# Key, value and expert-weight transfers laid out in other runs, and the token sort done through DRAM: one inference step on one core

## The reference

```python
h = modulate(rmsnorm(x, g_attn), shift, scale)
fq, fk, fv, logf, mq, mk, mv = project(h, w_in, b_forget)
o = merge_groups(fox(...), moba(...), g_out_fox, g_out_moba, w_out)   # 8 + 8 heads of 64
x = x + gate * o
h = modulate(rmsnorm(x, g_ffn), shift2, scale2)
# top-1 of 4 groups, then top-2 of the 8 experts in it; expert e on row h:
y_e = (silu(h @ w1[e]) * (h @ w3[e])) @ w2[e]      # w1, w3: 1024x256, w2: 256x1024
x = x + gate2 * (weighted sum of the two y_e);  y = rmsnorm(x, g_final)
```

## Time and profile before

| | us |
|---|---|
| runs | 919.58, 927.25, 929.08 |
| median | 927.25 |
| profiled execution | 922.37 |
| its span | 920.6 |
| PE busy | 675.6 |
| DVE busy | 398.9 |
| granted TensorE clock, mean | 0.832 |

### The profile page before, as it was taken

How to read it: one execution, slowest core, us unless ns; L and a number is a source line. 1 busy time by engine, 2 the same in 40 slices (tenths; PEclk the granted TensorE clock), 3 DMA queues, 4 the chain that set the end, 5 groups by cost and what they waited for, 6 DMA issues and landing times.

```text
span 920.6 us, 13094 instructions
## 1 busy us (share of the span) xinstructions
PE 675.6 (73%) x4650; PEld 376.1 (41%) x4650; DVE 398.9 (43%) x824; ACT 171.3 (19%) x438; POOL 170.0 (18%) x209
## 2 busy tenths in 40 slices
PE   4699999966464666566668978997777777687740
PEld 2356466444232333233335765444343434343410
DVE  1412112155877577576874237123323232323226
ACT  2011002048121111111202123121101111111013
POOL 2201203330044444454420000010000000000010
PEclk9899999977776765776769977999988898988885
DMA  9996779560585966866478080009999999999944
GB/s 324 405 379 185 278 297 365 184 240 1 167 296 208 320 222 203 322 218 211 129 262 275 1 275 0 1 29 369 378 369 378 368 378 368 378 369 378 370 127 131
DMA packets 126700, 233.77 MB, mean 254 GB/s; under 512 B 8626, under 2 KB 74347, under 8 KB 126532
## 3 DMA queue, kind: packets, MB, share of 16 engines
q1 hardware_dynamic: 105330, 176.70, 53.9%
q0 software_dynamic: 13232, 41.27, 13.8%
q10 hardware_dynamic: 8098, 15.28, 4.8%
HBM read 217.96 MB, written 15.25 MB: 253 GB/s over the span
## 4 chain that ended last, share of the span: by engine, by line
PE 32%; SPq 25%; DVE 21%; DMA 6%; issue 6%; another core or an unknown queue 5%; ACT 2%; ACTq 0%; DVEq 0%; POOL 0%; POOLq 0%
SPq L478 13%; SPq L479 11%; PE ps L1588 8%; DVE work L1144 5%; PE ps L1592 5%; PE ps L1885 4%; PE ps L1810 4%; DMA ring<-w_in 3%; SPq L477 2%; DVE p_half L1215 2%; PE ps L1898 2%; PE ps L1483 2%; PE ps L1692 1%; DMA ring<-w 1%
## 5 line engine op out<-in xcount | busy, mean ns | idle before, releaser
L1898 PE MATMUL ps<-ring,work 128*64 128x256 f32 x1024 | 148.6, 455 | 40.7 <-DMA ring<-w 39.5
L1898 PEld LDWEIGHTS ps<-ring,work 128*64 128x64 f32 x1024 | 87.4, 164 | 94.3 <-issue 70.8
L1383 DVE TENSOR_SCALAR work<-work 128x128 f32<-128x128 f32 x32 | 15.7, 490 | 214.4 <-ACT work L837 214.4
L1692 PE MATMUL ps<-work 128*32 128x256 f32 x512 | 55.5, 580 | 52.5 <-DVE work L1144 52.5
L563 POOL DMA_INDIRECT ring<-cache_moba_v,v_row x64 | 60.5, 946 | 140.1 <-PE ps L1737 116.5
L586 POOL COPY work<-work 128x512 f32 x32 | 19.6, 614 | 337.2 <-PE ps L1898 240.8
L1588 PE MATMUL ps<-xh,ring 128*128 128x320 f32 x256 | 73.7, 447 | 6.3 <-DMA ring<-w_in 6.3
L563 POOL DMA_INDIRECT ring<-cache_fox_v,v_row x64 | 60.7, 948 | 90.4 <-PE ps L1483 38.2
L1144 DVE STREAM_TRANSPOSE work<-ring 128x2048 f32<-128x2048 f32 x32 | 71.8, 2285 | 0.0
L1588 PEld LDWEIGHTS ps<-xh,ring 128*128 128x128 f32 x256 | 49.7, 197 | 28.7 <-DMA ring<-w_in 6.6
L1907 PE MATMUL ps<-ring,work 128*64 128x512 f32 x256 | 60.6, 593 | 0.7 <-ACT work L841 0.4
(11 more groups left out here) (318 smaller groups left out, 867.1 us busy)
## 6 DMA issues: line engine op xcount, KB each, us to landing
ring<-w SPq DMA_DIRECT2D x96, 1024.0 KB, 12.7
ring<-w_ada SPq DMA_DIRECT2D x4, 4096.0 KB
ring<-cache_fox_k SPq DMA_DIRECT2D x64, 256.0 KB
ring<-cache_moba_k SPq DMA_DIRECT2D x64, 256.0 KB
ring<-w_ada SPq DMA_DIRECT2D x4, 2048.0 KB, 13.8
ring<-w_in SPq DMA_DIRECT2D x2, 4096.0 KB
scr_y<-work ACTq DMA_DIRECT2D x64, 128.0 KB, 5.6
ring<-w_in SPq DMA_DIRECT2D x2, 2048.0 KB
```

The lines of the kernel that those rows point to most:

```text
L1692: last = mm(o.rearrange("p (q n) -> p q n", q=2), q_cur[:, u.g, 2 * h + e, :], ktv[:, :, 2 * h + e, :], start=(e == 0), stop=(e == 1))
L1898: last = mm(o, h_cur[:, par, c, :], w[:, c, f], start=(c == 0), stop=(c == KC - 1))
```

## The change

1. **Keys.** Token 4l + t of a page now goes to partition 32t + l. The transfer's DRAM side is therefore a pattern of 4 by 32 rows of 512 floats (outer step one row, inner step four rows); the SBUF side stays 128 partitions of 512.
2. **Values.** Partition 32a + l takes tokens 4l to 4l+3 of page a as one run of 8 KB, so that a unit has two indirect transfers in place of eight. The log-forget values, the bias tables and the suffix sums follow the new order of tokens.
3. **Expert weights.** w1 and w3 are loaded with eight neighbouring input rows per partition, one run of 8 KB, and each has a region of its own in the slot.
4. **Sort.** DVE casts the places to integers, POOL scatters the rows of `h_tok` to `scr_h` in DRAM with six indirect transfers, SP reads the sorted rows back in two transfers, and PE turns them with 40 transposes, which ACT and DVE evacuate. The one-hot matrices, their matmuls and POOL's iota go.
5. **Router.** The logits of the two prompt tiles are accumulated chunk by chunk as the activations come, into banks of their own; only the sample tile is left for the end. Some semaphores are merged.

```diff
--- before.py
+++ after.py
@@ -129,6 +129,7 @@
+    scr_h = nc.dram_tensor("scr_h", (ASSIGN, D), F32).ap()
@@ -148,7 +149,9 @@
-        w13_of = [s[:, 0:2 * KC * DE].rearrange("p (k n) -> p k n", k=KC) for s in eslot]
+        w1_of = [s[:, 0:KC * DE].rearrange("p (k n) -> p k n", k=KC) for s in eslot]
+        w3_of = [s[:, KC * DE:2 * KC * DE].rearrange("p (k n) -> p k n", k=KC) for s in eslot]
+        w13_of = [s[:, 0:2 * KC * DE].rearrange("p (a k f n) -> p k f a n", a=2, k=KC, f=FC) for s in eslot]
@@ -221,8 +224,7 @@
-        place1 = region(8704, 3 * ASSIGN).rearrange("p (t n) -> p t n", t=3)
-        iota_s = region(10624, ASSIGN)
+        h_rows = region(5632, ASSIGN // P * D).rearrange("p (j d) -> p j d", j=ASSIGN // P)
@@ -440,8 +443,8 @@
                 for a, page in enumerate(pages):
-                    sp.dma_start(kd[:, a, :], cache_k[u.g][0, bass.ds(page, 1)].rearrange("r t h d -> (r t) (h d)")
-                                 ).then_inc(ring_in[u.slot], 16)
+                    rows = cache_k[u.g][0, bass.ds(page, 1)].rearrange("r (l t) h d -> t (r l) (h d)", t=4)
+                    sp.dma_start(kd[:, a, :], rows).then_inc(ring_in[u.slot], 16)
@@ -461,8 +464,8 @@
             def load_expert(e, k, inc):
-                sp.dma_start(w13_of[k][:, :, 0:DE], w1[0, e].rearrange("(k p) n -> p k n", p=P)).then_inc(inc, 16)
-                sp.dma_start(w13_of[k][:, :, DE:], w3[0, e].rearrange("(k p) n -> p k n", p=P)).then_inc(inc, 16)
+                sp.dma_start(w1_of[k], w1[0, e].rearrange("(p k) n -> p k n", p=P)).then_inc(inc, 16)
+                sp.dma_start(w3_of[k], w3[0, e].rearrange("(p k) n -> p k n", p=P)).then_inc(inc, 16)
                 sp.dma_start(w2_of[k], w2[0, e].rearrange("(k p) n -> p k n", p=P)).then_inc(inc, 16)
@@ -470,12 +473,17 @@
+            sp.wait_ge(S["h_out"], 16 * 6)
+            hv = scr_h.rearrange("(j p) d -> p j d", p=P)
+            sp.dma_start(h_rows[:, 0:2], hv[:, 0:2]).then_inc(S["h_in0"], 16)
+            sp.dma_start(h_rows[:, 2:], hv[:, 2:]).then_inc(S["h_in1"], 16)
+
             def load_expert_dyn(e, k, inc):
-                sp.dma_start(w13_of[k][:, :, 0:DE], expert_at(w1, e, "o (k p) n -> p (o k) n")).then_inc(inc, 16)
-                sp.dma_start(w13_of[k][:, :, DE:], expert_at(w3, e, "o (k p) n -> p (o k) n")).then_inc(inc, 16)
+                sp.dma_start(w1_of[k], expert_at(w1, e, "o (p k) n -> p (o k) n")).then_inc(inc, 16)
+                sp.dma_start(w3_of[k], expert_at(w3, e, "o (p k) n -> p (o k) n")).then_inc(inc, 16)
                 sp.dma_start(w2_of[k], expert_at(w2, e, "o (k p) n -> p (o k) n")).then_inc(inc, 16)
@@ -556,13 +564,12 @@
                 vd = slot[u.slot][:, 4096:].rearrange("p (q t n) -> p q t n", q=2, t=4)
-                rows = cache_v[u.g][0].rearrange("r t h d -> (r t) (h d)")
+                rows = cache_v[u.g][0].rearrange("r (l t) h d -> (r l) (t h d)", t=4)
                 for q in range(2):
                     at = 2 * u.b + q
-                    for t in range(4):
-                        pool.indirect_dma_start(vd[:, q, t, :], None, rows,
-                                                bass.IndirectOffsetOnAxis(v_row[:, at:at + 1], 0),
-                                                element_offset=32 * t * W).then_inc(pages_v_in[u.slot], 16)
+                    pool.indirect_dma_start(vd[:, q].rearrange("p t n -> p (t n)"), None, rows,
+                                            bass.IndirectOffsetOnAxis(v_row[:, at:at + 1], 0)
+                                            ).then_inc(pages_v_in[u.slot], 16)
@@ -573,10 +580,14 @@
-            pool.wait_ge(S["wo_done"], 1)
-            nc.gpsimd.iota(iota_s, pattern=[[1, ASSIGN]], base=0, channel_multiplier=0,
-                           allow_small_or_imprecise_dtypes=True).then_inc(S["iota_done"], 1)
-            pool.wait_ge(S["sorted"], KC)
+            pool.wait_ge(S["htok_ev"], 12)
+            for a in range(2):
+                pool.wait_ge(S["slot"], a + 1)
+                for t, (_, n) in enumerate(TILES):
+                    pool.indirect_dma_start(scr_h, bass.IndirectOffsetOnAxis(slotu[0:n, 3 * a + t:3 * a + t + 1], 0),
+                                            h_tok[0:n, t, :], None).then_inc(S["h_out"], 16)
+            pool.wait_ge(S["sorted_a"], ASSIGN // P)
+            pool.wait_ge(S["sorted_v"], ASSIGN // P)
             pool.wait_ge(S["tabs"], 2)
@@ -818,19 +829,15 @@
-            for r in range(3):
+            for r in range(6):
-            for k in range(KC):
-                act.wait_ge(S["sort_mm"], k + 1)
-                nc.scalar.copy(h_sort[:, k, 0:512], ps[2 * (k % 2)][:, 0:512])
-                nc.scalar.copy(h_sort[:, k, 512:ASSIGN], ps[2 * (k % 2) + 1][:, 0:ASSIGN - 512]
-                               ).then_inc(S["sorted"], 1)
-            for r in range(3, 6):
-                gate_rows(r)
-            act.wait_ge(S["onehot"], 6)
-            act.wait_ge(S["sort_mm"], KC)
+            for j in range(ASSIGN // P):
+                act.wait_ge(S["sort_tp"], 2 * j + 1)
+                nc.scalar.copy(h_sort[:, 0:4, j * P:(j + 1) * P],
+                               ps[2 * (j % 2)][:, :].rearrange("p (k n) -> p k n", k=4)).then_inc(S["sorted_a"], 1)
+            act.wait_ge(S["sort_tp"], 2 * (ASSIGN // P))
-                          .rearrange("p o n -> p (o n)")).then_inc(S["gf_in"], 16)
+                          .rearrange("p o n -> p (o n)")).then_inc(par_in, 16)
@@ -993,7 +1000,7 @@
-                ts(v_row[rows, :], tables[rows, :].rearrange("p (g a) -> p g a", a=4)[:, :, a], float(PAGE),
+                ts(v_row[rows, :], tables[rows, :].rearrange("p (g a) -> p g a", a=4)[:, :, a], float(PAGE // 4),
@@ -1284,10 +1291,8 @@
-            br = brow[:].unsqueeze(1)
-            link(tt(lg[:, 0:2, :], ps[1][:, 0:72].rearrange("p (t n) -> p t n", t=2), br.broadcast_to([P, 2, 36]),
-                    ALU.add))
-            link(tt(lg[0:NS, 2, :], ps[1][0:NS, 72:108], brow[0:NS, :], ALU.add))
+            for t, (_, n) in enumerate(TILES):
+                link(tt(lg[0:n, t, :], ps[1 + t][0:n, 0:36], brow[0:n, :], ALU.add))
@@ -1326,14 +1331,8 @@
-
-            v.wait_ge(S["iota_done"], 1)
-            for t, (_, n) in enumerate(TILES):
-                ts(place1[0:n, t, :], iota_s[0:n, :], slots[0:n, 0, t:t + 1], None, ALU.is_equal
-                   ).then_inc(S["onehot"], 1)
-                v.wait_ge(S["onehot"], 2 * t + 1)
-                stt(place1[0:n, t, :], iota_s[0:n, :], slots[0:n, 1, t:t + 1], place1[0:n, t, :], ALU.is_equal,
-                    ALU.add).then_inc(S["onehot"], 1)
+                nc.vector.tensor_copy(slotu[:, 3 * a:3 * a + 3], slots[:, a, :]
+                                      ).then_inc(S["slot"], 1)
@@ -1375,6 +1374,11 @@
+            for j in range(ASSIGN // P):
+                v.wait_ge(S["sort_tp"], 2 * j + 2)
+                nc.vector.tensor_copy(h_sort[:, 4:8, j * P:(j + 1) * P],
+                                      ps[2 * (j % 2) + 1][:, :].rearrange("p (k n) -> p k n", k=4)
+                                      ).then_inc(S["sorted_v"], 1)
@@ -1838,12 +1842,13 @@
-            pe.wait_ge(S["h2_prompt"], KC)
+            for k in range(KC):
+                pe.wait_ge(S["h2_prompt"], k + 1)
+                for t, (t0, n) in enumerate(TILES[0:2]):
+                    mm(ps[1 + t][0:n, 0:36], hT[:, k, t0:t0 + n], wr[:, k, :], start=(k == 0), stop=(k == KC - 1))
             pe.wait_ge(S["h2_normed"], KC + 1)
-            for t, (t0, n) in enumerate(TILES):
-                for k in range(KC):
-                    last = mm(ps[1][0:n, 36 * t:36 * t + 36], hT[:, k, t0:t0 + n], wr[:, k, :],
-                              start=(k == 0), stop=(k == KC - 1))
+            for k in range(KC):
+                last = mm(ps[3][0:NS, 0:36], hT[:, k, NP:], wr[:, k, :], start=(k == 0), stop=(k == KC - 1))
             last.then_inc(S["r_mm"], 1)
@@ -1872,26 +1877,24 @@
                    start=True, stop=True).then_inc(S["gt_mm"], 1)
-            for r in range(3):
+            for r in range(6):
                 gate_rows(r)
-            for k in range(KC):
-                if k >= 2:
-                    pe.wait_ge(S["sorted"], k - 1)
-                for lo, hi, bank in ((0, 512, 2 * (k % 2)), (512, ASSIGN, 2 * (k % 2) + 1)):
-                    for t, (_, n) in enumerate(TILES):
-                        if k == 0 and lo == 0:
-                            pe.wait_ge(S["onehot"], 2 * t + 2)
-                        last = mm(ps[bank][:, 0:hi - lo], h_tok[0:n, t, k * P:(k + 1) * P], place1[0:n, t, lo:hi],
-                                  start=(t == 0), stop=(t == 2))
-                last.then_inc(S["sort_mm"], 1)
-            for r in range(3, 6):
-                gate_rows(r)
+            for j in range(ASSIGN // P):
+                pe.wait_ge(S["h_in0" if j < 2 else "h_in1"], 16)
+                if j >= 2:
+                    pe.wait_ge(S["sorted_a"], j - 1)
```

(37 more changed lines are left out.)

4 lines of the change are left out of this document (2 added, 2 removed).

## The result

The changed kernel takes 1000.43 us in the median of four runs (995.35 to 1002.28), the kernel before 923.41 in the runs taken beside it (919.51 to 929.08): a ratio of 1.082, with a 95% interval of 1.074 to 1.090. It is slower, and 998 had been forecast. The profiled execution took 1000.19 us, with a span of 998.4 (before 922.37 and 920.6), 77.8 more.

The account below looks back on a forecast made before the run. Prediction: attention bound by a DVE and PE chain, the sort by PE, experts by weight DMA; four engines loading keys become attention's bound. 922.4 + 116 (keys) - 17 (router and sort) - 23 (experts) = 998 us, range 950 to 1055.

Parts of the forecast that it names:

- Keys on four engines: Sample attention: key loads run on 4 of 16 engines, 26.0 us per unit against 15.6, +116 us.
- The store of the earlier trace: Store with an 8 by 32 pattern, share 0.51 at 100 GB/s, taken as sign that engines equal outermost steps.
- Values: Sample attention: 64 fewer gathers per group come off POOL, which then waits longer for PE; 0 us.
- the chain's 15.6 us per unit: Sample attention: pace of the DVE and PE chain before the change, from first to last key turns.
- spread-keys rival: Sample attention: keys stay spread over engines, attention keeps its 257 us, total 882 us; chance 0.15.
- from eight engines up: Sample attention: with eight engines keys and values take 15.6 us per unit, what the chain takes, so no loss.
- Router: Router: 32 products follow ACT's writes, 16 more end at 549.3 in place of 553.0; -3.7 us.
- Sort: Sort: scatter, read-back and transposes replace 36.7 us of PE; first expert at 589, -17 us including the router.
- Experts: Expert stretch: all weights at 408 GB/s, 0.83 us less for each of 28 experts, -23 us.
- the ceiling: Expert stretch: largest gain allowed for the weight loads, 27 us at 417 GB/s.
- Sum: Whole kernel: 922.4 + 116 - 17 - 23 = 998 us.

Follow-up runs that it names:

- e1: Kernel before with only the key loads' source taken 4 x 32 as in the change: 1043.24 us, ratio 1.125.
- e3: Changed kernel with the key loads' source taken 8 x 16 in place of 4 x 32: 875.08 us, ratio 0.943.
- e5: Changed kernel with the whole change in sample attention undone, keys and values; router, sort and experts as changed: 876.70 us, ratio 0.949.
- e2: Changed kernel with only the key loads' source put back to 128 rows in a row: 847.51 us, ratio 0.916.
- e6: Kernel before with only the values gathered as rows of four tokens, two gathers per unit in place of eight: 898.48 us, ratio 0.976.
- e7: Changed kernel with keys as 128 rows in a row and six tiny gathers more per unit, eight in all: 876.27 us, ratio 0.948.
- e10: Kernel before with only the changed router order and the scattered sort with read-back: 901.06 us, ratio 0.976.
- e9: Kernel before with only the experts' w1 and w3 loaded as 8 KB runs: 898.93 us, ratio 0.973.
- e12: Changed kernel with keys as 128 rows in a row and two tiny gathers more per unit, four in all: 848.09 us, ratio 0.918.
- e8: Changed kernel with keys as 128 rows in a row and values loaded by SP, one transfer per page, without gathers: 861.07 us, ratio 0.935.

## Why the prediction was right, and where not

- **Keys on four engines, +116: right.** e1 measures 116 for that line alone, and a unit takes 26.6 us there, 27.0 to 27.3 in the change, for 26.0. With keys alone in flight the share is 0.26 at 101 GB/s, and 0.53 at 203 with eight outermost steps. The store of the earlier trace rows was the right witness. e3 shows the rule at another count. The Trainium skill (DMA: Bandwidth & Descriptors, "Why a DMA increments its semaphore by 16 and not by 1") states it as the largest number up to 16 that divides the outermost dimensions; four and eight agree with the paces measured. The change lost 8 more than the term said, and its last keys were turned 6 us later than e1's; why is not settled.
- **Values, 0: right for the sum, wrong as a statement.** Keys set the pace in the changed kernel, so nothing that the values do shows there. But the reason given, that POOL only waits longer for PE, overlooked what POOL's gathers do to others: 29 us with keys out of the way (e5 against e2, e6, e7). It had been readable: DVE's and ACT's waits put down to "remote" beside back-to-back gathers. I had read the chain's 15.6 us per unit (16.7 in its steady part) as fixed.
- **The spread-keys rival, 882: mis-sized.** It came out at 847.5 in e2, for that reason. Its point of decision, "from eight engines up", was too low as well: against a chain of 14.4 us eight are still the bound, and cost 28 us (875.1 against 847.5).
- **Router, -3.7: right.** From DVE's first step on the rows' statistics (L955 at 662.59, before L948 at 536.02) to the last product it takes 12.9 us in place of 17.0.
- **Sort, with the router -17: right in sum.** Scatters issue at 1.3 us, forecast 1.25. The last is landed 3.9 us after its issue, where I took 5.9; the read-back takes 8.8 us, for 8.7; the first expert follows 14.7 us behind the start of the read-back, for about 15.5. Measured 18.2 with the router, and 21.3 in e10's trace, where PE's granted clock was higher.
- **Experts, -23: mis-sized.** 28.2 in the change, 26 in e9. The term that was too small is the rate: 420 GB/s, above the 408 I took, which no row has, and the 417 of the ceiling. (By the prediction's own terms 417 gives 28 us, not 27.) The bound of the Trainium skill (same page, "Where 436 GB/s comes from") of some 358 GB/s per core is contradicted by the window at 420, with this one core at work.
- **Sum.** The three parts are additive: e9 and e10 give 26 and 24, together 50, and e5 has 48. With attention's gain they leave 847.5, to which the keys' pattern adds 153. That the total came out within 2 us is partly luck: in the profiled execution the loss was 8 us larger than forecast and the two gains together 6 larger, and these cancel.

What stays open: what a gather instruction does to PE. The traces show that PE's results are taken up about 2 us late, and gaps of PE for which nothing is waited for, around POOL's last gathers of a unit. Of the 18 waits in the sample attention of the kernel before that are put down to "remote", 16 end 0.9 to 1.9 us behind the end of the eighth gather. Overlap alone does not do it: at 448.82 a result of PE comes during the seventh gather, and DVE takes it up 0.03 us later. e7 shows that the instructions and not their bytes do it, e12 that four are harmless where they stand. Whether it is PE's own instruction supply or the signal on its way was not tried.

## What to carry to other kernels

Before a transfer's pattern is reordered, count its outermost step on both sides: a count of 4 took a quarter of the engines here (share 0.26), and the bytes that share them have to be added before it is compared with the pace of the chain. A queue entry or an instruction that "only waits" can still cost: look for waits with no named releaser beside it, and test it with empty copies of itself, as e7 did. Where a change has parts that sit behind one bound, each part's worth is only seen with that bound taken away.

## What the runs showed of the hardware

- Key loads with 4, 8 and 128 outermost steps made units of 27, 17 and 14.4 us, with the same rows of 2 KB. Alone in flight, those with 4 kept 0.26 of the engines busy at 101 GB/s, those with 8 kept 0.53 at 203.
- Eight gather instructions of 0.95 us per unit added 29 us over the 16 units; six of the eight moved next to nothing in e7; four added nothing.
- Weight loads: 374 GB/s with 1 KB runs for two thirds of the bytes, 412 with 4 KB, 420 with 8 KB.
- In e8 transfers of four 2 KB rows into each of 32 partitions moved 219 GB/s with the engines full, those of one 2 KB row into each of 128 partitions 384.
- SP issued a load, of 256 KB or of 64 KB, in 0.5 us when the engines kept up, and in 2.6 us (20.70 / 8) when four engines had to drain it.
